# A two-block transformer kernel on one core: the products that only keep TensorE busy are taken out

## What is computed

```python
# first block
mod = silu(c) @ w_ada + b_ada                      # shift, scale, gate for both halves
h = rms_norm(x, norm1_gain) * (1 + sc1) + sh1
proj = h @ w_in                                    # 4864 columns
x = x + g1 * (merged(hgrn2(proj), attention(proj)) @ w_out)
h2 = rms_norm(x, norm2_gain) * (1 + sc2) + sh2
x = x + g2 * moe_ffn(h2)                           # router, top 4 of 32 experts, 1024 wide
# second block
proj = rms_norm_2(x, norm_mix_g) @ w_in_2          # 5120 columns
x = x + merged(stick_breaking(proj), conv(proj)) @ w_out_2
x = x + hierarchical_moe(rms_norm_2(x, norm_ffn_g))  # top 1 of 4 groups, top 2 of its 8 experts, 256 wide
```

## Time and profile before

| | |
|---|---|
| median of 3 runs | 1562.67 us (1560.21 to 1562.7) |
| the profiled execution | 1558.39 us |
| its span | 1556.6 us |
| mean granted clock of TensorE, share of full | 0.983 |
| TensorE busy | 1451.0 us (93%), 8700 matmul records |
| VectorE busy | 602.3 us (39%) |
| ScalarE busy | 342.8 us (22%) |
| HBM read | 592.66 MB, 381 GB/s over the span |

### The profile page before, as it was taken

The page is one execution under the profiler, slowest core; times in us unless marked ns, Lnnn a source line. Parts: engine busy times, 40 slices in busy tenths (PEclk is TensorE's granted clock), DMA queues, the critical chain, the costliest instruction groups (busy, mean ns, idle before and its releaser), DMA issues.

```text
span 1556.6 us, 20914 instructions
## 1 busy us (share of the span) xinstructions
PE 1451.0 (93%) x8700; PEld 757.0 (49%) x8700; DVE 602.3 (39%) x920; ACT 342.8 (22%) x395; POOL 22.7 (1%) x36
## 2 busy tenths in 40 slices
PE   5999999999999999998998989999989999997677
PEld 2878985333323333332332333333338999853343
DVE  3786683232213132321322321323247697422111
ACT  3564332010101010100100100101033474321110
POOL 1100100000000000000000000000000000000000
PEclk9999999999999999999999999999999999999889
DMA  9987589999999999999999999999996447999998
GB/s 382 367 324 276 198 353 398 428 429 429 429 428 425 428 429 428 429 428 427 429 428 428 428 427 429 428 427 428 428 403 218 163 163 287 364 385 423 422 422 316
DMA packets 76832, 594.63 MB, mean 382 GB/s; under 512 B 5434, under 2 KB 6688, under 8 KB 37348
## 3 DMA queue, kind: packets, MB, share of 16 engines
q1 hardware_dynamic: 74448, 588.25, 91.6%
q0 software_dynamic: 1792, 4.86, 0.9%
q10 hardware_dynamic: 532, 0.64, 0.1%
HBM read 592.66 MB, written 1.06 MB: 381 GB/s over the span
## 4 chain that ended last, share of the span: by engine, by line
PE 60%; DMA 35%; DVE 4%; issue 1%; ACT 1%; SPq 0%; DVEq 0%; ACTq 0%
PE PS L563 53%; DMA ring<-in_w_up 26%; DMA ring<-in_w_up_e 7%; PE PS L739 3%; DMA ring<-in_w_ada 1%; PE PS L1514 1%; DVE ring_r L361 1%; PE PS L763 1%; DVE arena L838 1%; PE PS L679 1%; ACT ring_r L356 0%; PE PS L1591 0%; DVE arena L2110 0%; DVE ring_r L1996 0%; DVE small L2101 0%
## 5 line engine op out<-in xcount | busy, mean ns | idle before, releaser
L563 PE MATMUL PS<-ring,arena 128*64 128x512 f32 x3020 | 670.7, 596 | 39.4 <-DMA ring<-in_w_up 27.2
L563 PEld LDWEIGHTS PS<-ring,arena 128*64 128x64 f32 x3020 | 212.4, 137 | 460.0 <-issue 400.7
L563 PE MATMUL PS<-arena 128*128 128x128 f32 (+12 forms) x1240 | 228.9, 441 | 3.7 <-ACT arena L559 1.4
L826 DVE TENSOR_SCALAR arena<-PS 128x512 f32<-128x512 f32 x32 | 22.1, 692 | 480.6 <-PE PS L563 480.6
L542 ACT ACTIVATE arena<-arena 128x512 f32<-128x512 f32 x32 | 20.2, 630 | 696.5 <-DVE arena L826 696.5
L563 PE MATMUL PS<-ring_r 128*128 128x256 f32 (+1 forms) x576 | 170.9, 304 | 0.4 <-DVE ring_r L1996 0.4
L563 PEld LDWEIGHTS PS<-arena 64*128 64x128 f32 (+6 forms) x1240 | 108.6, 164 | 121.3 <-issue 114.7
L563 PE MATMUL PS<-hT_r,ring_r 128*128 128x256 f32 x800 | 150.3, 284 | 0.4 <-DVE ring_r L361 0.4
L361 DVE TENSOR_TENSOR ring_r<-ring,ring_r 128x2048 fp32r<-128x2048 f32 x51 | 116.4, 2291 | 34.9 <-ACT ring_r L356 33.8
L563 PEld LDWEIGHTS PS<-hT_r,ring_r 128*128 128x128 f32 x800 | 126.6, 192 | 2.3 <-issue 1.4
L356 ACT ACTIVATE ring_r<-ring 128x2048 fp32r<-128x2048 f32 x51 | 97.2, 1912 | 102.5 <-PE PS L563 98.5
(11 more groups left out here) (382 smaller groups left out, 974.1 us busy)
## 6 DMA issues: line engine op xcount, KB each, us to landing
ring<-in_w_up SPq DMA_DIRECT2D x128, 2048.0 KB, 21.0
ring<-in_w_down SPq DMA_DIRECT2D x59, 2048.0 KB, 18.8
ring<-in_w_in SPq DMA_DIRECT2D x17, 2048.0 KB, 11.5
ring<-in_w_gate_e SPq DMA_DIRECT2D x14, 2048.0 KB, 19.3
ring<-in_w_down_e SPq DMA_DIRECT2D x13, 2048.0 KB, 20.9
ring<-in_w_up_e SPq DMA_DIRECT2D x13, 2048.0 KB, 19.4
ring<-in_w_ada SPq DMA_DIRECT2D x12, 2048.0 KB, 15.8
ring<-in_w_out SPq DMA_DIRECT2D x4, 2048.0 KB, 7.8
```

The source lines that it names most:

```text
L563: return nc.tensor.matmul(o, w, m, start=first, stop=last)
L826: V.tensor_scalar(glu.rearrange("p (kk b q) -> p kk b q", kk=4, b=2), hu[:, :, :, :, 0], 7.0, None, ALU.min)\
```

## The change

Both helpers and all nine calls go; nothing else is touched. The waits around them stay.

```diff
-        def keep_warm_short(n, bank):
-
-            for _ in range(n):
-                mm(PS[:, bank, 0:P], ident, ident, True, True)
-
-        def keep_warm(n, bank):
-
-
-            for _ in range(n):
-                mm(PS[:, bank, :], ident, consts[:, 0:512], True, True)
...
                 if last and i == 1:
                     pe.wait_ge(S(f"{X}_added"), 2 * it + 2)
-                    keep_warm(6, 7)
...
-            if last:
-                keep_warm(2, 7)
             arrived(pe, 4)
...
             last.then_inc(S("mod1"), 1)
-            keep_warm_short(6, 7)
             first_tokens()
             ada(4)
             pe.wait_ge(S("hT_V"), 1)
             split_tokens(1)
-            keep_warm_short(6, 4)
             split_cols(2)
...
             last.then_inc(S("logits"), 1)
-            keep_warm_short(8, 7)
             positions_mm(pe, "n2")
-            keep_warm_short(5, 7)
...
-            keep_warm(4, 2)
             transpose_h(pe, "n3")
...
             last.then_inc(S("logits"), 1)
-            keep_warm_short(12, 7)
             positions_mm(pe, "n4")
-            keep_warm_short(4, 7)
             pe.wait_ge(S("hT_A"), 10)
             moe2_gather(pe, "m2", 0)
```

## The result

The changed kernel is slower: 1568.64 us, the median of 6 runs (1566.64 to 1570.81), where the kernel before took 1561.25 us beside it (6 runs, 1560.21 to 1562.7). The ratio is 1.0047, 95% interval [1.0036, 1.0058], or +7.3 us [5.6, 9.1]. The forecast said 1566.6 us in a range of 1562.0 to 1571.5 us, slower, on a median before of 1562.67 us.

A forecast was written before the change was run, and what follows sets the result against it. TensorE was taken to bound the mixers and DMA the expert stages. Terms 1.3 - 1.26 + 1.2 + 0.5 + 1.9 + 0.5 = +4.1 us on the 1562.67 us median gave 1566.8, stated as 1566.6 us, range 1562.0 to 1571.5 us.

The forecast's parts named there:

- What bounds the kernel, and what passes through the expert stage: TensorE bounds the mixers, DMA the expert stages; TensorE time lost before 250 us or between 1150 and 1357 us stays lost.
- the transfers hide it: Rival, chance 0.08: DMA queue has enough in hand at 250 us, so losses before it vanish; +2.9 us, 1565.6 us.
- Site 1: Opening, first six warming products: without them the real products start cold and must earn the clock; +1.3 us.
- Site 2: Opening, second six warming products: they stand in an unbroken stretch, so removal saves their time; -1.26 us.
- Site 3: First router chain, eight and five products ahead of the first experts: clock falls around positions and gather; +1.2 us, ends 0 and 5.
- it stays cold longer: Rival, chance 0.14: a cold gather may not bring the clock back before the expert products; +10 us, 1572.7 us.
- Site 4: Start of the second block, four wide products: cold transposes, partly covered by waits; +0.5 us, ends 0 and 2 us.
- Site 5: Second router chain, twelve and four products ahead of the second experts: gather partly cold; +1.9 us, ends 0 and 4 us.
- Site 6: Last group: six wide products out cost 2.1 us, two in line return 1.92 us, further fall +0.3 us; net +0.5 us.
- The further fall under the last products: Last group: in one case of three the clock falls again for about 1 us in the thinned stretch; +0.3 us.
- The rival on weight loads: Rival, chance 0.05: weight loads ignore the granted clock, so cold gathers keep 0.12 us per record; +1.6 us, 1564.3 us.
- Faster, -3.2 us: Rival, chance 0.05: only the in-line products count, 1.26 us in the opening and 1.92 us in the last group; 1559.5 us.

The follow-up runs named there:

- e1_router1: Only the thirteen warming products of the first router chain taken out of the kernel before: 1.0020 [1.0011, 1.0029], +3.1 us.
- e5_first: Only the first six warming products of the opening taken out of the kernel before: 1.0003 [0.9992, 1.0015], +0.5 us.
- e10_keep8: Kernel before without the five products behind the first router chain's positions; the eight ahead stay: 1.0019 [1.0006, 1.0031], +3.0 us.
- e3_mid: Only the four wide products ahead of the second block's transposes taken out of the kernel before: 1.0004 [0.9995, 1.0013], +0.6 us.
- e4_inline: Kernel before without the products in line (second six of the opening, two wide ones in the last group): 0.9978 [0.9968, 0.9987], 1557.83 us.
- e9_best: Kernel before without the products in line, with eleven warming products added ahead of ada(3) in the opening: 0.9986 [0.9976, 0.9996], -2.2 us.
- e2_router2: Only the sixteen warming products of the second router chain taken out of the kernel before: 1.0015 [1.0005, 1.0024], +2.3 us.
- e6_last6: Only the six wide warming products of the last group taken out of the kernel before: 1.0014 [1.0003, 1.0025], +2.2 us.
- e12_last_both: Both warming calls of the last group taken out of the kernel before: 1.0007 [0.9997, 1.0016], +1.1 us.
- e13_open_both: Both warming calls of the opening taken out of the kernel before: 1.0005 [0.9996, 1.0014], +0.8 us.
- e11_plus5: Changed kernel with the five products between positions and gather of the first router chain put back: 1.0055 [1.0042, 1.0068] against the kernel before.

## Why the prediction was right, and where a size was off

- *What bounds the kernel, and what passes through the expert stage.* Right. The delay at 250 us is found again in full from there on, and the rival "the transfers hide it" fell with e1_router1.
- *Site 1*, +1.3 us: the trace had about +1.5 us, like compared with like, e5_first +0.5 us [-1.2, 2.3] by time. The trace shows the mechanism; that it costs time is not shown by itself. Its size depends on how long the real products stay cold, 3.5 us in one execution, 6 us in another.
- *Site 2*, -1.26 us: right to 0.1 us in the trace.
- *Site 3*, +1.2 us: the term that was mis-sized. It measured +3.1 us [1.7, 4.5], and 5.2 us in the trace. Two steps were wrong. I had about 3 us cold, spread over positions and gather; in the trace the gather was cold throughout, and so was most of the first expert's first products, that is, the rival "it stays cold longer" is what that execution shows at this site. And I took the two gaps together for the cause; in e10_keep8 the second alone did it, 1.1 us of idle time behind ten light records. The table of idle times on which I had leaned (2.3 us costs the clock, 1.8 us does not the earlier trace rows) was the wrong measure: the same idle time of about 3 us in the opening cost the clock in six traces and not in six others. What decides besides the length of the gap, the work around it or the moment at which it comes, was not separated by a run.
- *Site 4*, +0.5 us: measured +0.6 us [-0.8, 2.0]; 1.4 us in the trace of the changed kernel and 0.4 us in that of e3_mid, inside the ends.
- *Site 5*, +1.9 us: measured +2.3 us [0.8, 3.7], 2.5 us in the trace. Right. (3.4 x 0.10/0.22 is 1.5 us, not 1.6 us, which changes nothing.)
- *Site 6*, +0.5 us: measured +1.1 us [-0.5, 2.5]. The six cost 2.2 us when out, forecast 2.1 us. The further fall under the last products did not come in these traces. A wait for weights of 0.6 us took the place of part of the two products where only these were out (e4_inline, e9_best); the changed kernel, with its last products later, has none, so there the two gave back their full time.
- *The rival on weight loads.* It fell. The gather, whose records move 64 columns only, went from 3.98 to 7.09 us on the cold clock, with weight loads in progress for all of it (6.87 us of 6.90 us in the window from 242.7 us); its pace follows the clock. (The Trainium skill, *TensorE: Matmul & The Clock Gate*, section on LDWEIGHTS, gives one figure for a load, with no word of the clock; the measurement decides.)
- *Faster, -3.2 us.* As a forecast for this change it was rightly small; as a price of the products in line it fits the time of e4_inline, -3.4 us [-5.0, -2.0]. In part that is luck, for the trace gives 2.4 us at the two sites, and e9_best, without the same two, measured -2.2 us [-3.7, -0.6].

The sum was +4.1 us and the measurement +7.3 us; 3.2 us lie between them. By the parts, site 3 gives 1.9 us, the opening 0.8 us, site 6 0.6 us, site 5 0.4 us and site 4 0.1 us, in sum 3.8 us, within the noise of the whole. Only at site 3 does the forecast lie outside the interval of its part. The median of before lay 1.4 us below the one that I had started from, which brought the forecast time nearer than its sum was.

## What to carry to other kernels

Judge each product that only warms the engine by what stands behind it: one that fills a wait costs nothing and may protect everything up to the next wide stretch; one that stands in line costs its full time. Here the seven calls that fill waits earn their place or do not measurably cost, and the two in line cost 3.4 us [2.0, 5.0]. Look for the danger not only where TensorE idles, but where it works on narrow or short products. Take as the upper end of the price that the whole stage and the next wide products run cold; here that was 5.2 us in the trace, and 3.1 us over the runs. And do not read one trace as the rule: the clock falls in the same code in one execution and holds in the next.

## What was not expected of the hardware

- A fully busy TensorE lost its clock: 3.40 us of 3.40 us busy with 93 narrow records, then 0.50 for the next 3.4 us. It happened near 140 us in 8 of 13 profiled executions, e3_mid among them, where it lasted 6.8 us:

```profile
140.00:146.80 6.80, 6.80 (x57) 6.65 (x54) 6.55 (x13) 0.00 (x0) 0.00 (x0) 0.50 0.75 298
```

- So a kernel whose warming products are all in place loses its clock now and then as well: in the first router chain in e2_router2 and e6_last6, and in the second in e9_best, e12_last_both and e13_open_both. Each time the fall came ahead of the positions, the warming products ran slow, and the gather behind them ran at its full pace. In e2_router2 the eight took 3.39 us, not 2.03 us, and the gather 3.88 us. So the call that fills the wait also takes up a fall that comes before it. It fits that the kernel before spreads over 5 us in one set of runs (1558.98 to 1564.16 us, 33 runs) and 8 us in another (1557.44 to 1565.85 us, 35 runs), though the two were not tied together by a run. It was not tried to mend the stage at 140 us.
- A gather of light records can stay cold for its whole length: 32 records in 7.09 us, with the clock back only 3.3 us into the wide products of the first expert. It need not: in e11_plus5 the clock came back in the middle of the same gather:

```profile
246.50:247.00 0.50, 0.50 (x4) 0.50 (x4) 0.07 (x1) 0.00 (x0) 0.00 (x0) 0.50 1.15 459
247.50:248.00 0.50, 0.50 (x7) 0.50 (x6) 0.00 (x0) 0.00 (x0) 0.00 (x0) 1.00 0.65 279
```
